# A two-layer decoder trunk on one core: weight slots of 4112 bytes, and where operands start modulo 256

## The chip, the core and the metric

The kernel runs on one core of one Trainium2 chip. The metric is the device time in microseconds (us) from start to end of one execution. The profile names the engines PE (TensorE, matmuls), PEld (TensorE's weight loads, which overlap its matmuls), DVE (VectorE), ACT (ScalarE), POOL (GpSimd) and SP (SyncE, which here only issues DMAs). TensorE's clock was granted at 0.999 of its full 2.4 GHz over the profiled execution.

## What is computed

Two decoder layers over 512 tokens of width 1024, in float32. Layer 0 mixes tokens with a chunkwise mLSTM, layer 1 with differential attention; both attend to a memory of 256 tokens, and both end in a SwiGLU feed-forward part 2816 wide:

```python
for i in range(DEPTH):
    h = rmsnorm(x, norm1[i])
    mix, xq = mlstm_mixer(h, ...) if i % 2 == 0 else diff_attention(h, positions, ...)
    xo = memory_cross_attention(xq, mem, mem_norm[i], w_mem_kv[i], xq_norm[i], xk_norm[i])
    x = x + jnp.concatenate([mix, xo], axis=-1) @ w_out[i]
    h = rmsnorm(x, norm2[i])
    gu = h @ w_gate_up[i]
    x = x + (jax.nn.silu(gu[..., :FFN_HIDDEN]) * gu[..., FFN_HIDDEN:]) @ w_down[i]
```

## The kernel before

**Three products for one.** All big products (the input projections, w_out, gate and up, down) run on TensorE in the type float32r. To keep float32's precision, each weight tile and each activation tile is split into a rounded high part and the rest, and three matmuls stand for one: high weight by high activation, high weight by low activation, low weight by high activation. A weight tile is 128 output columns by up to 8 blocks of 128 rows. It comes by DMA into one of four raw slots (`w_raw`), POOL (or ACT and DVE) splits it into `w_hi` and `w_lo`, and PE reads it there.

**Dense tiles** (`tile`, line 1946 is the helper `mm`): for each of 8 blocks k, three matmuls of 128x512. The operand that streams through the array (the moving one) is `Hh[:, k]` or `Hl[:, k]` (the normed tokens) or `Ah[:, k]` or `Al[:, k]` (the mixers' and the feed-forward part's outputs); the operand that is loaded into it first is a 128x128 block of `w_hi` or `w_lo`. There are 3120 such matmuls, and 192 more with only 256 moving columns (the memory's keys and values). `slot_of(n)` says in which of three slots of `w_hi` and `w_lo` tile n stands; most tiles alternate between slots 0 and 1.

**Pairs** (`pair`, line 2284): 16 of the 22 hidden blocks of each layer compute gate and up together, as seven products of quarter size (a Strassen-like scheme) over sums of activations (`tc_hi`, `tc_lo`) and sums of weights. Each product q takes 4 blocks of weights, starting at block `4 * q` (q is permuted a little in layer 1), and each block takes three matmuls of 128x256: 84 a pair, 2688 in all. The 28 blocks of the seven products lie in the same memory as the three slots: blocks 0 to 7 in slot 0, 8 to 15 in slot 1, 16 to 23 in slot 2, and 24 to 27 behind it.

**What PE does meanwhile.** Every matmul needs its own weight load, and the next load runs while the present matmul streams. So TensorE reads two places of SBUF at once: the moving rows of matmul i, and the weights of matmul i + 1.

**Where the operands lie.** Tensors are placed in SBUF in the order in which the function `sb` is called, each at the next multiple of 32 bytes. All the big ones were a multiple of 256 bytes long, so that they start alike modulo 256 (addresses are bytes within a partition):

| tensor | start before | modulo 256 | start after | modulo 256 |
|---|---|---|---|---|
| Hh, Hl | 17536, 33920 | 128 | the same | 128 |
| Ah, Al | 50304, 66688 | 128 | 50400, 66784 | 224 |
| w_raw | 83072 | 128 | 83168 | 224 |
| w_hi, w_lo | 99456, 113792 | 128 | 99616, 114208 | 32 |
| tc_hi, tc_lo | 169152, 197824 | 192 | 169632, 198304 | 160 |
| cn (constants), ones | 128128, 132896 | 128, 32 | 128608, 133376 | 96, 0 |
| tmp0, tmp1 | 154688, 156768 | 64, 96 | 155168, 157248 | 32, 64 |

In this text the **distance** is the start of the moving operand less the start of the weights loaded meanwhile, modulo 256. The step from one block to the next is 512 bytes for weights and 2048 or 1024 for moving rows, so that within a tile the distance stays the same. Before, it is 0 for every dense matmul and 64 for every matmul of a pair.

The lines that the change touches: the allocation of `w_hi` and `w_lo` and their views (`wq_hi`, `wq_lo` by block, `w_hi`, `w_lo` by slot), and four places that read or write a quarter's blocks: `weight_low` on POOL (line 748) and on DVE (line 1704), `weight_hi` on ACT (line 1099) and the matmul in `pair` (line 2284).

Of the kernel before, what the change touches and what calls it, by code (L numbers as in the profile page):

```python
# [25 lines left out]
F32 = mybir.dt.float32  # L26
F32R = mybir.dt.float32r
I32 = mybir.dt.int32
ALU = mybir.AluOpType
ACT = mybir.ActivationFunctionType  # L30
AX = mybir.AxisListType

P = 128
# [25 lines left out]
SPLIT = 3  # L59
# [60 lines left out]
HI_ENTRY = [4, 6, 0, 1, 5, 2, 3]  # L120
TOKENS = 13
SHARED = 2


def bq_tile(c):
# [138 lines left out]
def hybrid_trunk(nc, x_t, mem_t, positions, wt, wg_cols, a_gate_b, b_lambda, prm_cols, con, out):  # L264
    ctx = ExitStack()
    with ctx:
        def sb(name, shape, dt=F32, scope=ctx):
            return scope.enter_context(nc.sbuf_tensor(name, shape, dt))
# [7 lines left out]
        xT = sb("xT", [P, KD, SEQ])  # L276
        Hh = sb("Hh", [P, KD, SEQ], F32R)
        Hl = sb("Hl", [P, KD, SEQ], F32R)
        Ah = sb("Ah", [P, 8, SEQ], F32R)
        Al = sb("Al", [P, 8, SEQ], F32R)  # L280
        w_raw = sb("w_raw", [P, RAW, 8, P])
        wq_hi = sb("w_hi", [P, 28, P], F32R)
        wq_lo = sb("w_lo", [P, 28, P], F32R)
        w_hi = wq_hi[:, 0:8 * SPLIT].rearrange("p (s k) m -> p s k m", k=8)
        w_lo = wq_lo[:, 0:8 * SPLIT].rearrange("p (s k) m -> p s k m", k=8)
        cn = sb("cn", [P, N_CON])
        ones = sb("ones", [P, P])
        gcol = sb("gcol", [P, N_PRM])
# [229 lines left out]
        s_round = sem("s_round")  # L518
# [68 lines left out]
        def pair_source(n, q):  # L587

            gate, up = w_raw[:, n % RAW], w_raw[:, (n + 1) % RAW]
            return (gate[:, 0:4], W_SUM[1], W_SUM[0], W_SUM[2], gate[:, 4:8], W_SUM[3], up[:, 4:8])[q]  # L590
# [106 lines left out]
        def _(pool):  # L697
# [6 lines left out]
            for i in range(4):  # L704
                w = slice(2 * i, 2 * i + 2)
# [14 lines left out]
            for i in range(0, 4, 2):  # L720
                w = slice(i, i + 2)
# [23 lines left out]
            def weight_low(n, p, q):  # L745
                b = block_of(pair_at(n)[0], q)
                pool.wait_ge(s_round, weight_round(p, q))
                nc.gpsimd.tensor_tensor(wq_lo[:, b:b + 4], pair_source(n, q), wq_hi[:, b:b + 4].bitcast(F32),  # L748
                                        ALU.subtract).then_inc(s_low_p, 1)

            for n in range(2, N_TILES):
# [11 lines left out]
                if after_pairs(n):  # L763
                    l, s = after_pairs(n)
# [35 lines left out]
        def _(act):  # L800
# [266 lines left out]
            def ffn(l):  # L1067
# [17 lines left out]
                def weight_hi(s, i, q):  # L1085

                    n, p, b = seg_base(l, s) + 2 * i, pair_number(l, s, i), block_of(l, q)
                    if q in (0, 4, 6):
                        m = n + (q == 6)
                        act.wait_ge(w_in[m % RAW], (m // RAW + (m % RAW > 0)) * 16)  # L1090
                    else:
                        act.wait_ge(s_add, 4 * p + {1: 2, 2: 1, 3: 3, 5: 4}[q])
                    if i and q == 6:
                        act.wait_ge(dense_done, n)
                    elif i:
                        act.wait_ge(product, 6 * (p - 1) + q + 1)
                    else:
                        act.wait_ge(dense_done, n - 1 + q // 2 if q < 4 else n - KD + 1)
                    nc.scalar.activation(wq_hi[:, b:b + 4], pair_source(n, q), ACT.Copy).then_inc(s_round, 1)  # L1099

                def shared_hi(n):

# [215 lines left out]
        def _(dve):  # L1318
# [330 lines left out]
            def ffn(l):  # L1649
# [50 lines left out]
                def weight_low(s, i, q):  # L1700

                    n, p, b = seg_base(l, s) + 2 * i, pair_number(l, s, i), block_of(l, q)
                    dve.wait_ge(s_round, weight_round(p, q))
                    nc.vector.tensor_tensor(wq_lo[:, b:b + 4], pair_source(n, q), wq_hi[:, b:b + 4].bitcast(F32),
                                            ALU.subtract).then_inc(s_low_v, 1)

                def pair(s, i):
# [236 lines left out]
        def _(pe):  # L1944
# [317 lines left out]
            def pair(l, s, i):  # L2262

                p = pair_number(l, s, i)
                for q in range(7):
                    if q in P_LO:
                        pe.wait_ge(s_low_p, len(P_LO) * p + P_LO.index(q) + 1)
                    else:
                        pe.wait_ge(s_low_v, low_count(p, q))
                    if q == 4:  # L2270
                        pe.wait_ge(gate_read, 2 * p + 1)
                    elif q > 4:
                        pe.wait_ge(joined, joined_of(p, q - 3))
                    elif p and q == 0:
                        pe.wait_ge(gate_read, 2 * p)
                    elif p and q == 3 and i > plain_pairs(s):
                        pe.wait_ge(dense_free, seg_base(l, s) + 2 * i)
                    elif p and q < 3:
                        pe.wait_ge(joined, joined_of(p - 1, (1, 4)[q - 1]))
                    out_ = PS[:, Q_BANK[q], 0:HALF_T]  # L2280
                    b = block_of(l, q)
                    for k in range(4):
                        for j, (w, a) in enumerate(((wq_hi, tc_hi), (wq_hi, tc_lo), (wq_lo, tc_hi))):
                            last = nc.tensor.matmul(out_, w[:, b + k], a[:, q, k], start=q < 4 and k == 0 and j == 0,  # L2284
                                                    stop=k == 3 and j == 2, skip_group_check=q > 3)
                    last.then_inc(dense_done if q == 6 else product, 2 if q == 6 else 1)

# [328 lines left out]
```

## Time and profile before

| | |
|---|---|
| time, median of 2 runs | 1202.85 us (1202.53 to 1203.17) |
| profiled execution | 1204.02 us, its span 1202.2 us |
| PE busy | 1196.8 us, 100% of the span |
| PEld busy | 1032.9 us, 86% |
| POOL busy | 857.4 us, 71% |
| DVE, ACT busy | 755.9 us, 63%; 502.4 us, 42% |
| DMA | 117.43 MB, mean 98 GB/s |

A row of a grouped view gives line, engine, operation, output and inputs by the program's names, the shape, the count, the total busy time and the mean duration of one. Matmuls overlap: one is recorded from its start until its last result is written, and the next has started long before. So a matmul's duration is longer than the time from one start to the next, and it is the second that adds up to the span.

### The profile page before, as it was taken

The numbers are of one execution on the slowest core, as the hardware profiler recorded it, in microseconds if no ns is written. First come the engines' busy times: TensorE is split into PE (matmuls) and PEld (weight loads), VectorE is DVE, ScalarE is ACT, GpSimd is POOL, SyncE is SP. The second block draws the span as 40 slices with busy tenths as digits, with TensorE's granted clock in tenths as the row PEclk, the third lists the DMA queues.
The fourth block names the chain that finished last, engine by engine and source line by source line (L and its number), as shares of the span: only waits on it lengthen the run. The fifth ranks groups of instructions, "written<-read, shape, count | busy, mean of one in ns | idle before, by whom it ended". The sixth has DMA issues, their size and how long they took to land.

```text
span 1202.2 us, 18736 instructions
## 1 busy us (share of the span) xinstructions
PE 1196.8 (100%) x6998; PEld 1032.9 (86%) x6998; DVE 755.9 (63%) x1099; ACT 502.4 (42%) x1012; POOL 857.4 (71%) x873
## 2 busy tenths in 40 slices
PE   9999999999999999999999999999999999999998
PEld 7888887788889998899888777778888899889997
DVE  7954434645737991599335888874674599348931
ACT  7522456733203551355231666644431255125510
POOL 7998433566878996699676444445688799669965
PEclk9999999999999999999999999999999999999999
DMA  7234211132223333233433222232232333322332
GB/s 282 92 123 157 71 36 53 53 106 79 92 83 106 106 106 123 88 106 106 126 103 97 80 71 71 64 80 69 71 100 79 118 106 107 105 89 98 115 105 85
DMA packets 35097, 117.43 MB, mean 98 GB/s; under 512 B 4417, under 2 KB 4930, under 8 KB 34886
## 3 DMA queue, kind: packets, MB, share of 16 engines
q1 hardware_dynamic: 33416, 112.83, 29.2%
q10 hardware_dynamic: 1598, 3.51, 1.2%
q8 instruction: 51, 0.84, 0.3%
q14 instruction: 32, 0.26, 0.1%
HBM read 111.07 MB, written 2.11 MB: 94 GB/s over the span
## 4 chain that ended last, share of the span: by engine, by line
PE 97%; DVE 1%; ACT 1%; issue 0%; ACTq 0%; POOL 0%; POOLq 0%
PE PS L1946 69%; PE PS L2284 26%; PE PS L2385 1%; DVE Al L1564 0%; PE PS L2194 0%; PE PS L2413 0%; PE PS L2354 0%; DVE nmB L1850 0%; PE PS L2019 0%; PE PS L2346 0%; PE PS L2338 0%; DVE PB L1862 0%; ACT tmp L1010 0%; ACT tmp L1018 0%; DVE PB L1861 0%
## 5 line engine op out<-in xcount | busy, mean ns | idle before, releaser
L783 POOL TENSOR_TENSOR w_lo<-w_raw,w_hi 128x256 fp32r<-128x256 f32 (+1 forms) x516 | 394.7, 796 | 11.0
L778 POOL TENSOR_SCALAR w_hi<-w_raw 128x1024 fp32r<-128x1024 f32 (+2 forms) x132 | 142.1, 1076 | 283.4 <-PE PS L1946 275.0
L2284 PE MATMUL PS<-tc_hi,w_hi 128*128 128x256 f32 x896 | 250.9, 280 | 0.0
L2284 PE MATMUL PS<-tc_hi,w_lo 128*128 128x256 f32 x896 | 250.0, 279 | 0.0
L2284 PE MATMUL PS<-tc_lo,w_hi 128*128 128x256 f32 x896 | 250.0, 279 | 0.0
L1946 PE MATMUL PS<-Hh,w_hi 128*128 128x512 f32 x560 | 229.3, 410 | 0.0
L1946 PE MATMUL PS<-Hl,w_hi 128*128 128x512 f32 x560 | 219.1, 391 | 0.0
L1946 PE MATMUL PS<-Hh,w_lo 128*128 128x512 f32 x560 | 219.0, 391 | 0.0
L1946 PE MATMUL PS<-Ah,w_hi 128*128 128x512 f32 (+1 forms) x544 | 208.0, 382 | 0.1
L1946 PE MATMUL PS<-Ah,w_lo 128*128 128x512 f32 (+1 forms) x544 | 205.0, 377 | 0.0
L1946 PE MATMUL PS<-Al,w_hi 128*128 128x512 f32 (+1 forms) x544 | 204.9, 377 | 0.0
L2284 PEld LDWEIGHTS PS<-tc_hi,w_lo 128*128 128x128 f32 x896 | 168.5, 188 | 0.0
L2284 PEld LDWEIGHTS PS<-tc_hi,w_hi 128*128 128x128 f32 x896 | 168.2, 188 | 0.2
L2284 PEld LDWEIGHTS PS<-tc_lo,w_hi 128*128 128x128 f32 x896 | 167.6, 187 | 0.2
L1619 DVE TENSOR_TENSOR xT<-xT,PS 128x512 f32<-128x512 f32 x64 | 43.9, 687 | 159.4 <-PE PS L1946 159.4
L1946 PEld LDWEIGHTS PS<-Hh,w_hi 128*128 128x128 f32 x560 | 105.6, 189 | 27.6 <-issue 7.8
L1946 PEld LDWEIGHTS PS<-Hh,w_lo 128*128 128x128 f32 x560 | 105.4, 188 | 22.8
L1946 PEld LDWEIGHTS PS<-Hl,w_hi 128*128 128x128 f32 x560 | 105.7, 189 | 20.2 <-issue 1.0
L748 POOL TENSOR_TENSOR w_lo<-tmp,w_hi 128x512 fp32r<-128x512 f32 x64 | 107.7, 1700 | 17.9 <-ACT w_hi L1099 17.9
L1946 PEld LDWEIGHTS PS<-Ah,w_hi 128*128 128x128 f32 x544 | 102.3, 188 | 20.7 <-issue 1.5
L1946 PEld LDWEIGHTS PS<-Ah,w_lo 128*128 128x128 f32 x544 | 102.3, 188 | 19.0
L1946 PEld LDWEIGHTS PS<-Al,w_hi 128*128 128x128 f32 x544 | 102.4, 188 | 18.6 <-issue 0.5
(300 smaller groups left out, 1805.5 us busy)
## 6 DMA issues: line engine op xcount, KB each, us to landing
w_raw<-in_wt_dram SPq DMA_DIRECT2D x181, 512.0 KB, 3.6
w_raw<-in_wt_dram SPq DMA_DIRECT2D x16, 384.0 KB, 3.0
w_raw<-in_wt_dram SPq DMA_DIRECT2D x8, 448.0 KB, 3.3
QKR<-QKP ACTq DMA_DIRECT2D x24, 128.0 KB, 4.8
xT<-in_x_t_dram SPq DMA_DIRECT2D x8, 256.0 KB, 4.8
out_dram<-xT SPq DMA_DIRECT2D x8, 256.0 KB, 2.0
mT<-in_mem_t_dram SPq DMA_DIRECT2D x1, 1024.0 KB, 9.5
cn<-in_constants_dram SPq DMA_DIRECT2D x1, 594.5 KB, 6.9
```

Source lines behind the costliest of these rows:

```text
L748: nc.gpsimd.tensor_tensor(wq_lo[:, b:b + 4], pair_source(n, q), wq_hi[:, b:b + 4].bitcast(F32), ALU.subtract).then_inc(s_low_p, 1)
L778: nc.gpsimd.tensor_scalar(w_hi[:, sl, 0:nk], w_raw[:, raw, 0:nk], 0.0, 1.0, ALU.add, ALU.mult).then_inc(w_round, 1)
L783: lo = nc.gpsimd.tensor_tensor(w_lo[:, sl, w], w_raw[:, raw, w], w_hi[:, sl, w].bitcast(F32), ALU.subtract)
L1619: nc.vector.tensor_tensor(xT[:, k], xT[:, k], PS[:, bank], ALU.add).then_inc(dense_free, 1)
L1946: return nc.tensor.matmul(out_, a, b, start=start, stop=stop)
L2284: last = nc.tensor.matmul(out_, w[:, b + k], a[:, q, k], start=q < 4 and k == 0 and j == 0, stop=k == 3 and j == 2, skip_group_check=q > 3)
L2385: last = nc.tensor.transpose(PS[:, 2 + u % 2, k * P:(k + 1) * P], PB[:, 0, W_OFF[u] + k * P:W_OFF[u] + (k + 1) * P], ident)
```

## The change

The change puts three unused tensors between the operands (96 bytes ahead of `Ah`, 64 ahead of `w_hi`, 192 ahead of `w_lo`), and makes the weight slots 4112 bytes long instead of 4096, so that slot s starts 16 s bytes later modulo 256. The quarters of a pair keep their blocks, and follow the slots. With that the distances are:

| moving operand | before | after, slot 0, 1, 2 |
|---|---|---|
| Hh, Hl | 0 | 96, 80, 64 |
| Ah, Al | 0 | 192, 176, 160 |
| tc_hi, tc_lo (blocks 0-7, 8-15, 16-23, 24-27) | 64 | 128, 112, 96, 80 |

No instruction is added or taken away, and on no engine does one move: the order of instructions, their shapes and their waits are the same. Only addresses differ, those of the tensors behind `w_lo` too (all by 480 bytes).

```diff
+W_STEP = 8 * P + 4
...
         Hl = sb("Hl", [P, KD, SEQ], F32R)
+        sb("shift_a", [P, 24])
         Ah = sb("Ah", [P, 8, SEQ], F32R)
         Al = sb("Al", [P, 8, SEQ], F32R)
         w_raw = sb("w_raw", [P, RAW, 8, P])
-        wq_hi = sb("w_hi", [P, 28, P], F32R)
-        wq_lo = sb("w_lo", [P, 28, P], F32R)
-        w_hi = wq_hi[:, 0:8 * SPLIT].rearrange("p (s k) m -> p s k m", k=8)
-        w_lo = wq_lo[:, 0:8 * SPLIT].rearrange("p (s k) m -> p s k m", k=8)
+        sb("shift_hi", [P, 16])
+        wf_hi = sb("w_hi", [P, SPLIT * W_STEP + 4 * P], F32R)
+        sb("shift_lo", [P, 48])
+        wf_lo = sb("w_lo", [P, SPLIT * W_STEP + 4 * P], F32R)
+
+        def tile_slots(ap):
+
+            full = ap[:, 0:SPLIT * W_STEP].rearrange("p (s x) -> p s x", x=W_STEP)
+            return full[:, :, 0:8 * P].rearrange("p s (k m) -> p s k m", m=P)
+
+        def quarter_blocks(ap):
+
+            first = [(b // 8) * W_STEP + (b % 8) * P for b in range(0, 28, 4)]
+            return [ap[:, f:f + 4 * P].rearrange("p (k m) -> p k m", m=P) for f in first]
+
+        w_hi, w_lo = tile_slots(wf_hi), tile_slots(wf_lo)
+        wq_hi, wq_lo = quarter_blocks(wf_hi), quarter_blocks(wf_lo)
...
-                            last = nc.tensor.matmul(out_, w[:, b + k], a[:, q, k], start=q < 4 and k == 0 and j == 0,
+                            last = nc.tensor.matmul(out_, w[b // 4][:, k], a[:, q, k], start=q < 4 and k == 0 and j == 0,
```

The other edits write `wq_hi[b // 4]` for `wq_hi[:, b:b + 4]`, and the same for `wq_lo`, in the three places named above.

## Rows read from the trace of the kernel before

**Rows 1.** The page: busy time by engine, and the chain that ended last.
```profile
PE 1196.8 (100%) x6998; PEld 1032.9 (86%) x6998; DVE 755.9 (63%) x1099; ACT 502.4 (42%) x1012; POOL 857.4 (71%) x873
...
PE 97%; DVE 1%; ACT 1%; issue 0%; ACTq 0%; POOL 0%; POOLq 0%
```

**Rows 2.** The chain in order of time (start us, us, what): its longest pieces.
```profile
377.26 79.15 PE PS L2284 x672
456.41 43.56 PE PS L1946 x192
```

**Rows 3.** PE's groups, shapes apart, whole span: count, busy us, mean ns.
```profile
L1946 PE MATMUL PS<-Al,w_hi 128*128 128x256 f32 x64 | 18.1, 282 | 0.0
...
L1946 PE MATMUL PS<-QK 128*128 128x256 f32 x12 | 3.2, 379 | 0.0
L1946 PE MATMUL PS<-Hh,wg 128*128 128x512 f32 x8 | 3.2, 404 | 0.0
...
L1946 PE MATMUL PS<-QK,KZ 128*128 128x256 f32 x4 | 1.2, 379 | 0.0
```

**Rows 4.** The same, 300 to 324 us: dense tiles of gate and up alone.
```profile
L1946 PE MATMUL PS<-Hh,w_lo 128*128 128x512 f32 x36 | 14.0, 389 | 0.0
L1946 PE MATMUL PS<-Hh,w_hi 128*128 128x512 f32 x36 | 14.0, 389 | 0.0
L1946 PE MATMUL PS<-Hl,w_hi 128*128 128x512 f32 x36 | 14.0, 389 | 0.0
```

**Rows 5.** The same, 380 to 455 us: pairs alone.
```profile
L2284 PE MATMUL PS<-tc_hi,w_hi 128*128 128x256 f32 x213 | 59.6, 280 | 0.0
L2284 PE MATMUL PS<-tc_hi,w_lo 128*128 128x256 f32 x213 | 59.4, 279 | 0.0
L2284 PE MATMUL PS<-tc_lo,w_hi 128*128 128x256 f32 x213 | 59.4, 279 | 0.0
```

**Rows 6.** The same, 283.19 to 283.3 us: the last matmuls before `ones` is loaded.
```profile
L1946 PE MATMUL PS<-Hh,w_lo 128*128 128x512 f32 x1 | 0.4, 397 | 0.0
L1946 PE MATMUL PS<-Hl,w_hi 128*128 128x512 f32 x1 | 0.4, 389 | 0.0
```

**Rows 7.** The same, 651.7 to 651.8 us: the last before `tmp1` is loaded.
```profile
L1946 PE MATMUL PS<-Hh,w_lo 128*128 128x512 f32 x1 | 0.4, 396 | 0.0
```

**Rows 8.** The same, 650.1 to 650.2 us: the last before `tmp0` is loaded.
```profile
L1946 PE MATMUL PS<-Hh,w_lo 128*128 128x512 f32 x1 | 0.4, 388 | 0.0
```

**Rows 9.** The same, 456.2 to 458.1 us: the first dense matmuls behind the pairs.
```profile
L1946 PE MATMUL PS<-Ah,w_hi 128*128 128x512 f32 x3 | 1.2, 398 | 0.0
L1946 PE MATMUL PS<-Al,w_hi 128*128 128x512 f32 x3 | 1.2, 388 | 0.0
L1946 PE MATMUL PS<-Ah,w_lo 128*128 128x512 f32 x2 | 0.8, 394 | 0.0
```

**Rows 10.** Stretches: POOL's busy us (count), clock, DMA share, GB/s, in pairs.
```profile
380.00:450.00 70.00, 66.56 (x43) 1.00 0.30 106
```

More of the change, by code:

```diff
@@ L747, in weight_low @@
                 pool.wait_ge(s_round, weight_round(p, q))
-                nc.gpsimd.tensor_tensor(wq_lo[:, b:b + 4], pair_source(n, q), wq_hi[:, b:b + 4].bitcast(F32),
+                nc.gpsimd.tensor_tensor(wq_lo[b // 4], pair_source(n, q), wq_hi[b // 4].bitcast(F32),
                                         ALU.subtract).then_inc(s_low_p, 1)
@@ L1098, in weight_hi @@
                         act.wait_ge(dense_done, n - 1 + q // 2 if q < 4 else n - KD + 1)
-                    nc.scalar.activation(wq_hi[:, b:b + 4], pair_source(n, q), ACT.Copy).then_inc(s_round, 1)
+                    nc.scalar.activation(wq_hi[b // 4], pair_source(n, q), ACT.Copy).then_inc(s_round, 1)
                 def shared_hi(n):
@@ L1703, in weight_low @@
                     dve.wait_ge(s_round, weight_round(p, q))
-                    nc.vector.tensor_tensor(wq_lo[:, b:b + 4], pair_source(n, q), wq_hi[:, b:b + 4].bitcast(F32),
+                    nc.vector.tensor_tensor(wq_lo[b // 4], pair_source(n, q), wq_hi[b // 4].bitcast(F32),
                                             ALU.subtract).then_inc(s_low_v, 1)
```

## The prediction

> **What bounds the kernel now.** I read the page first: PE is busy for 1196.8 of 1202.2 us, and 97% of the chain that ended last is PE [rows 1]. So the time is the sum of the steps from one matmul's start to the next, and no other engine's speed matters as long as it stays under PE's. The change touches addresses alone. It can therefore move the time only through how long such a step takes, and the next views are there to measure it.
>
> The chain in order of time gives it directly. 192 dense matmuls take 43.56 us, 226.9 ns each; 672 matmuls of pairs take 79.15 us, 117.8 ns each [rows 2]. The grouped views give the same steps in another form. A dense matmul is recorded with 389 ns [rows 4] and one of a pair with 279 to 280 [rows 5]: both are the step plus 162 ns, the time from the last column's entry to the last result. So 162 ns off a recorded duration gives the step, also for a single matmul. At 2.4 GHz (the clock granted here is 1.00) 512 columns take 213.3 ns and 256 take 106.7. What is over, I call the surplus:
>
> - dense, 512 columns, distance 0: 226.9 - 213.3 = about 13.5 ns;
> - dense, 256 columns, distance 0: 282 - 162 - 106.7 = about 13.3 ns [rows 3];
> - pairs, 256 columns, distance 64: 117.8 - 106.7 = 11.1 ns.
>
> The first two say that the surplus does not grow with the columns: it belongs to the weight load, one a matmul. The last two differ in the tensors and in the distance, and by 2.3 ns. For comparison, plain float32 matmuls stream each column for twice as long: 256 columns take 379 - 162 = 217 ns, 213.3 and 3.7 more by this reckoning, and the same at distance 0 (`QK` by `QK`) and at 192 (`QK` by `KZ`) [rows 3]. So there is no effect of the distance where the moving rows come at half the speed, and for float32r some 10 ns of a surplus of 11 to 13.5 could in principle be saved.
>
> **The change part by part.** The sum is made against the profiled execution, whose span is 1202.2 us; its own time is 1204.02, and the median of the runs shown is 1202.85, so I add each term to 1202.85.
>
> *Dense matmuls away from distance 0.* There are 3312. If a distance other than 0 gives them the pairs' surplus, each saves 2.3 ns: 3312 x 2.3 = 7.6 us less. Bounds: at best the surplus falls to that of float32, 10 ns less each, 33 us; at worst it is that of the single loads below.
>
> *Distance 96.* Single loads show other distances. When `ones` (distance 96) is loaded under a matmul with `Hh`, that matmul is recorded with 397 ns, its neighbour with 389 [rows 6]; it is so at all four places where this load stands in a stretch of dense tiles, of which one is shown. `tmp1` (distance 32) gives 396 [rows 7], `tmp0` (distance 64), behind the same instructions, 388 [rows 8]. So 64 is good and 32 and 96 cost 8 ns more. By the table of slots, 718 dense loads (H tiles in slot 0) and 768 loads of pairs (blocks 16 to 23) come to distance 96. Were every one 8 ns longer, that is 1486 x 8 = 11.9 us more. But a single step is not a steady one. Behind the pairs the distance is 0 at once, yet the first eight steps read 398, 388 and 394 ns [rows 9], and then 389: the stall depends on what went before, and settles. I take half, 6 us more, and keep 0 and 12 as bounds.
>
> *Pairs leave distance 64.* They go to 128, 112, 96 and 80. If they fell to distance 0's surplus, 2688 x 2.3 = 6.2 us more; if they keep theirs, 0. The one row at distance 128 is the load of `wg` under `Hh`, 404 ns [rows 3], in the kernel's first 16 us, where every load is disturbed. I take 0.
>
> *Slots that differ.* Where the distance changes by 16 from tile to tile, and four times in a pair, the steps may have to settle anew. In the whole program the weights' start modulo 256 now changes 248 times between neighbours. Rows 9 price one settling: 3 x 398 + 3 x 388 + 2 x 394 - 8 x 389 = 34 ns [rows 9], for a change of shape and of 64 bytes. 248 x 34 ns = 8.4 us is the upper bound, 0 the lower; with a step of only 16 bytes I take 2.
>
> *Everything else.* ACT, DVE and POOL write and read the same number of bytes at shifted addresses, and the DMA's rows are as long as before. I cost it at nothing: in the dense tiles PE runs without a gap, and all of these engines have slack there. The pairs are the exception: POOL is busy for 66.56 of 70 us [rows 10]. A pair can get shorter by no more than 4.9% before PE waits for POOL, which caps what pairs could give at 2688 x 117.8 ns x 0.049 = 15.5 us. A POOL that got 5% slower by its new addresses would hold the pairs up; nothing in the rows speaks for that.
>
> Sum: -7.6 + 6 + 0 + 2 = 0.4 us, 1203 us.
>
> **A rule of the skill.** The rows say that a matmul's surplus goes with the weight load and was 2.3 ns smaller at distance 64 [rows 2, 3]. The Trainium skill, "TensorE: Matmul & The Clock Gate", section "What happens when you issue a matmul", states that TensorE has two independent SBUF read ports and that loading the next tile's weights doesn't steal read bandwidth from the running matmul. By it the distance would be of no account, and the sum would be 0. The rows agree for float32 and not quite for float32r.
>
> **The rivals.**
>
> *Most of the stall goes.* The two reads collide at distance 0 in a way that the new distances avoid. For it: a surplus of 13.5 ns against float32's 3.7 [rows 3, 4], and one that varies with the distance at all. Against: distance 64 is away from 0 and saves only 2.3 ns; no step in the steady stretches is shorter. Price: 33 us in the dense tiles, 15.5 in the pairs (POOL's cap): 1154 us; half of it 1179. It is faster by over 2% as soon as the mean step falls by 4 ns over the 6000 float32r matmuls. Chance 0.19.
>
> *The new distances stall more.* The 8 ns of rows 6 and 7 are steady, and hold for 80, 176 and 192 too. For it: distances 32 and 96 are the only ones in these rows that are far from 0 and 64, and both are bad; the settled state of distance 0 is then a lucky one. Against: 388 ns at distance 64 [rows 8]. Price: 6000 x 8 ns = 48 us, 1251 us; it decides (over 2% slower) from a mean of 4 ns on, 1227. Chance 0.13.
>
> *The address is of no account.* Steps of dense matmuls and pairs differ for another reason (the tensors' place in SBUF, or the pattern of the products), and rows 6 and 7 are particular to float32 weights. Then nothing moves: 1202.85 us. Chance 0.18.
>
> *The forecast:* small effects of both signs, 1190 to 1220 us. Chance 0.50.
>
> **How the numbers follow.** Over 2% is 24 us, about what a measurement of this kernel can tell from no change. Faster by over 2%: 0.19; slower: 0.13; within 2%: 0.50 + 0.18 = 0.68. The predicted time is the forecast's sum, 1203 us. For eight in ten the range takes in the nearer half of each outer rival: from 1168 us (a mean step 6 ns shorter) to 1226. The likeliest case's own range is 1190 to 1220.
>
> **What the profile would show.** Instructions, their order, the chain's shares (97% PE) and POOL's load stay. The dense groups in a stretch of gate and up tell the first two terms: 387 ns in place of 389 if a distance other than 0 gives the pairs' surplus, 397 in the tiles of slot 0 with H if distance 96 costs 8 ns steadily, 379 if the stall goes. A tiles (192, 176) and H tiles (96, 80) will differ if the distance matters. The pairs' 279 to 280 ns tell the third; a first matmul in each tile that is longer than the later ones, the fourth. The prediction is wrong if the mean moves by over 4 ns, or if PE starts to wait for POOL's w_lo in the pairs.

## The result, and the profile after

The changed kernel takes 1219.47 us (median of 2 runs, 1218.67 to 1220.26) against 1202.85 us: a ratio of 1.0138, with an interval of 1.0109 to 1.0168. So it is 16.6 us slower, a difference under the 2% that the prediction's cases are divided by, and outside the noise. The profiled execution took 1220.26 us, its span is 1218.5 us at a granted clock of 0.999.

The page of after (busy time by engine, then the chain that ended last by engine) answers to [rows 1]:

```profile
PE 1213.1 (100%) x6998; PEld 1036.0 (85%) x6998; DVE 741.6 (61%) x1099; ACT 504.8 (41%) x1012; POOL 855.2 (70%) x873
...
PE 98%; DVE 1%; DMA 0%; POOL 0%; ACT 0%; issue 0%; ACTq 0%; SPq 0%; POOLq 0%
```

Same instructions, and the chain is still PE's for 98%: PE's busy time has grown by 16.3 us and the span by 16.3. The pieces of the chain in order of time (start, us, what) answer to [rows 2]:

```profile
381.72 80.16 PE PS L2299 x672
461.88 44.62 PE PS L1961 x192
```

672 matmuls of pairs went from 79.15 to 80.16 us, 117.8 to 119.3 ns a step. 192 dense ones with `A` went from 43.56 to 44.62 us, 226.9 to 232.4 ns. The grouped view of 470 to 500 us, dense tiles with `A` alone (PE's groups, shapes apart: count, busy us, mean ns; idle before), has 395 ns where [rows 4] have 389:

```profile
L1961 PE MATMUL PS<-Al,w_hi 128*128 128x512 f32 x44 | 17.4, 395 | 0.0
L1961 PE MATMUL PS<-Ah,w_lo 128*128 128x512 f32 x44 | 17.4, 395 | 0.0
```

With `H` the two slots can be told apart in the view of one line's instructions of after (306 to 309 us, a tile in slot 0, distance 96; durations as least/median/most), and in the grouped view of 300 to 304 us (a tile in slot 1, distance 80):

```profile
L1961 PE MATMUL PS<-Hl,w_hi x5: 399/399/399, 305.7 to 308.5; 128*128 128x512 f32 x5
L1961 PE MATMUL PS<-Hh,w_lo x5: 392/392/397, 305.9 to 308.7; 128*128 128x512 f32 x5
L1961 PE MATMUL PS<-Hh,w_hi x5: 392/394/394, 306.1 to 308.9; 128*128 128x512 f32 x5
```
```profile
L1961 PE MATMUL PS<-Hh,w_lo 128*128 128x512 f32 x7 | 2.7, 392 | 0.0
L1961 PE MATMUL PS<-Hl,w_hi 128*128 128x512 f32 x6 | 2.4, 393 | 0.0
L1961 PE MATMUL PS<-Hh,w_hi 128*128 128x512 f32 x6 | 2.4, 392 | 0.0
```

The three matmuls of a block are now unequal and repeat: 399, 394, 392 at distance 96. Their mean less 162 is 233; at distance 80 it is 230. And the pairs, whole span, against 279 to 280 in [rows 5]:

```profile
L2299 PE MATMUL PS<-tc_lo,w_hi 128*128 128x256 f32 x896 | 253.0, 282 | 0.0
L2299 PE MATMUL PS<-tc_hi,w_lo 128*128 128x256 f32 x896 | 252.6, 282 | 0.0
L2299 PE MATMUL PS<-tc_hi,w_hi 128*128 128x256 f32 x896 | 252.5, 282 | 0.0
```

Adding up the steps from start to start, out of the start times of all PE instructions in both traces (neighbouring pairs of matmuls on `w_hi` or `w_lo` whose step is under 300 ns), gives where the time came from:

| matmuls | before: distance, steps, mean ns | after: distance, mean ns | us |
|---|---|---|---|
| `A`, 512 columns | 0, 1404, 227.1 | 192: 233.1; 176: 231.8; 160: 233.3 | +7.6 |
| `H`, 512 columns | 0, 1475, 227.9 | 96: 233.5; 80: 230.3; 64: 229.3 | +5.6 |
| `A`, 256 columns | 0, 187, 120.9 | 192: 117.4; 176: 119.8; 160: 117.5 | -0.5 |
| pairs, 256 columns | 64, 2688, 117.8 | 128: 118.7; 112: 119.8; 96: 119.5; 80: 118.4 | +3.7 |

Together +16.5 us, for 16.3 of the span; all other steps together got 0.2 us shorter. So the whole loss is in the steps of float32r matmuls, and most of it in the dense tiles. Of the 5.6 us of `H`, 3.7 fall on the tiles at 96 (658 of the steps), and 1.8 on those at 80 and 64.

### The profile page after: what moved, and what is told of

It reads as the page before. It is cut to its first block, busy times and chain, and to the rows that moved or that the text cites. A ratio compares the mean times of both kernels' runs of the same rounds, so it can differ in the third digit from the quotient of the medians.

```text
span 1218.5 us, 18736 instructions
## 1 busy us (share of the span) xinstructions
PE 1213.1 (100%) x6998; PEld 1036.0 (85%) x6998; DVE 741.6 (61%) x1099; ACT 504.8 (41%) x1012; POOL 855.2 (70%) x873
## 4 chain that ended last, share of the span: by engine, by line
PE 98%; DVE 1%; DMA 0%; POOL 0%; ACT 0%; issue 0%; ACTq 0%; SPq 0%; POOLq 0%
PE PS L1961 69%; PE PS L2299 26%; PE PS L2400 1%; PE PS L2209 0%; PE PS L2428 0%; DMA w_raw<-in_wt_dram 0%; PE PS L2369 0%; DVE nmB L1865 0%; PE PS L2034 0%; PE PS L2361 0%; PE PS L2353 0%; DVE PB L1877 0%; PE PS L2169 0%; PE PS L2172 0%; DVE PB L1876 0%; DVE PS L1863 0%
## 5 line engine op out<-in xcount | busy, mean ns | idle before, releaser
L2299 PE MATMUL PS<-tc_lo,w_hi 128*128 128x256 f32 x896 | 253.0, 282 | 0.0
L2299 PE MATMUL PS<-tc_hi,w_lo 128*128 128x256 f32 x896 | 252.6, 282 | 0.0
L1961 PE MATMUL PS<-Al,w_hi 128*128 128x512 f32 (+1 forms) x544 | 207.4, 381 | 0.0
```

What stands on the lines that cost most here:

```text
L1961: return nc.tensor.matmul(out_, a, b, start=start, stop=stop)
L2299: last = nc.tensor.matmul(out_, w[b // 4][:, k], a[:, q, k], start=q < 4 and k == 0 and j == 0, stop=k == 3 and j == 2, skip_group_check=q ...
```

## The experiments

Two theories at first. **Distance:** the step of a float32r matmul depends on the distance of its moving rows from the weights that are loaded meanwhile, modulo 256. **Place:** it depends on where one operand lies by itself (modulo 256, or in SBUF), or on the slots that differ by 16 bytes; then shifting everything, or one side, would do as much. Edits are against the kernel before unless another is named.

### Everything shifted alike: all_moved

```diff
+        sb("shift_all", [P, 40])
         xT = sb("xT", [P, KD, SEQ])
```

> The kernel before with one unused tensor of 160 bytes ahead of everything: Hh, Ah and the weights all start at 32 modulo 256, where the changed kernel's weights start; the distances stay 0 (dense) and 64 (pairs). Distance theory: 1203 us, dense matmuls 389 ns, pairs 279 to 280. Place theory (weights at 32 are what costs): about as slow as the changed kernel, 1219, dense matmuls 394 or more.

1202.70 us, ratio 0.9999 (0.9987 to 1.0010). All operands lie 160 bytes further on, no distance changed, and the durations stayed within 1 ns (grouped view, whole span):

```profile
L2285 PE MATMUL PS<-tc_hi,w_lo 128*128 128x256 f32 x896 | 250.0, 279 | 0.0
...
L1947 PE MATMUL PS<-Hh,w_lo 128*128 128x512 f32 x560 | 218.8, 391 | 0.0
...
L1947 PE MATMUL PS<-Ah,w_lo 128*128 128x512 f32 x480 | 186.9, 389 | 0.0
```

A shift of everything by 160 bytes is of no account.

### Only H against its weights: ahead_of_a

```diff
+        sb("shift_a", [P, 24])
         Ah = sb("Ah", [P, 8, SEQ], F32R)
```

`A` and the weights move together by 96 bytes, so `A` stays at 0 and the pairs at 64, while `H`'s distance becomes 160.

> One part of the change alone: 96 bytes ahead of Ah. A and the weights move together, so only H tiles change their distance, from 0 to 160; A stays at 0 and the pairs at 64. Distance theory: A tiles 389 ns and pairs 279 to 280 as before; H tiles at the changed kernel's figure for distance 160, a step of about 233, recorded 395: 1680 matmuls x about 6 ns = 10 us more, 1213. Place theory (Ah at 224 is what costs): A tiles slower, H tiles not.

1211.77 us, ratio 1.0075 (1.0045 to 1.0104). Whole span, grouped:

```profile
L1947 PE MATMUL PS<-Hh,w_lo 128*128 128x512 f32 x560 | 221.8, 396 | 0.0
...
L1947 PE MATMUL PS<-Ah,w_lo 128*128 128x512 f32 x480 | 186.9, 389 | 0.0
```

`H` rose from 391 to 396 ns and `A` stayed at 389, though `A` and the weights had moved and `H` had not. `H`'s mean step is 234.0 ns, 6.1 more than before; by the 1475 steps that is 9.0 us, and the kernel lost 9.1. That is distance, not place.

### The changed kernel without slots of 4112 bytes: no_slot_step

```diff
-W_STEP = 8 * P + 4
+W_STEP = 8 * P
...
-        sb("shift_lo", [P, 48])
+        sb("shift_lo", [P, 64])
...
+        sb("shift_cn", [P, 16])
```

(Against the kernel after.) All slots now lie alike: `H` at 96, `A` at 192, pairs at 128.

> The change with slots of 4096 bytes again and everything else of it: all H tiles at distance 96, all A tiles at 192, all pairs at 128, no change of the distance between neighbours. Distance theory: each group reads what it reads at that distance in the changed kernel, steps of 233.5 (H), 233 (A) and 118.7 (pairs): 3 ns more on the half of the H matmuls that were at 80, 1 ns more on A's at 176, 1 ns less on three quarters of the pairs: about 1219, like the changed kernel. Slot theory (it is the changes between neighbours that cost): most of the 16 us comes back, 1203 to 1208.

1222.80 us, ratio 1.0166 (1.0137 to 1.0196), 3.3 us above the changed kernel where the same had been expected. The steps themselves came as expected: `H` 233.4 ns, `A` 233.3, pairs 118.7. So the loss needs no steps between slots; with them it is even less, since slot 1's distances 80 (230.3) and 176 (231.8) are better than 96 and 192.

### The distances measured by themselves: probe

The model is left out but for a copy of x; PE alone runs series of 48 float32r matmuls, three for each of 8 blocks, twice, as in a tile. Each series has one pair of offsets, at 512 or 256 columns (the generator of one series; its first lines are left out):

```diff
+            for r in range(2):
+                for k in range(8):
+                    for j, (W, o, M) in enumerate(((Wh, wo, Mh), (Wh, wo, Ml), (Wl, wl, Mh))):
+                        yield (PS[:, r, 0:n], W[:, o + k * P:o + (k + 1) * P], M[:, mo + k * n:mo + (k + 1) * n],
+                               k == 0 and j == 0, k == 7 and j == 2)
```

> This kernel leaves out all of the model: it copies x to the output, and PE runs nothing but series of 48 dense-like matmuls (two tiles of 24, in the three-product pattern), each series from a source line of its own. Series 1 to 18: 512 columns, the weights moved by 0, 0, then 0 to 240 bytes in steps of 16 with the moving rows fixed (distance 0 downwards: 0, 240, 224, ...). Then the same 16 with 256 columns. Then 8 with the moving rows moved by 0 to 224 in steps of 32 and the weights fixed (distance upwards), then three with both moved by 32, 96 and 160 (distance 0), then distance 0 again. The distance theory (the step from one matmul to the next depends on the moving operand's start less the weights', modulo 256, and on nothing else of the place): the recorded durations at 512 columns are 389 ns at distance 0 in all places, about 392 to 396 at 64 to 192 as in the changed kernel's tiles (step 230 at 80, 233 at 96, 232 at 176, 233 at 192, plus 162), and a series with the moving rows moved equals the one with the weights moved the other way. The place theory (where weights or rows start modulo 256 or 64 matters, each for itself): the last three series differ from 389, and the two sweeps don't mirror each other. If both are wrong and the change slowed PE through the other engines' traffic, all series read the same.

It took 442.67 us, clock 1.00. Rows of the grouped view (one line of code is one series; 512 columns): line 319 at distance 0, 323 at 192, 329 at 96, 331 at 64, all four by an offset of the weights; 354 at 96 by an offset of the moving rows; 360 with both offset by 96.

```profile
L329 PE MATMUL PS<-Mh,Wh 128*128 128x512 f32 x16 | 6.4, 399 | 0.0
L354 PE MATMUL PS<-Ml,Wh 128*128 128x512 f32 x16 | 6.4, 399 | 0.0
...
L323 PE MATMUL PS<-Ml,Wh 128*128 128x512 f32 x16 | 6.3, 396 | 0.0
...
L331 PE MATMUL PS<-Mh,Wh 128*128 128x512 f32 x16 | 6.3, 394 | 0.0
...
L329 PE MATMUL PS<-Mh,Wl 128*128 128x512 f32 x16 | 6.3, 394 | 0.0
...
L329 PE MATMUL PS<-Ml,Wh 128*128 128x512 f32 x16 | 6.3, 392 | 0.0
L331 PE MATMUL PS<-Mh,Wl 128*128 128x512 f32 x16 | 6.3, 392 | 0.0
...
L319 PE MATMUL PS<-Mh,Wh 128*128 128x512 f32 x16 | 6.2, 389 | 0.0
...
L360 PE MATMUL PS<-Ml,Wh 128*128 128x512 f32 x16 | 6.2, 389 | 0.0
...
L331 PE MATMUL PS<-Ml,Wh 128*128 128x512 f32 x16 | 6.2, 388 | 0.0
```

399, 394, 392 at 96: the same three numbers as in the changed kernel's tile. It does not matter which operand is moved, and moved together they are back at 389. No other engine works during these series, so the two reads of PE are enough to make it. The settled mean steps, from start to start, in ns:

| distance | 0 | 16 | 32 | 48 | 64 | 80 | 96 | 112 | 128 | 144 | 160 | 176 | 192 | 208 | 224 | 240 |
|---|---|---|---|---|---|---|---|---|---|---|---|---|---|---|---|---|
| 512 columns | 226.7 | 226.7 | 233.3 | 233.3 | 228.9 | 229.8 | 233.4 | 233.4 | 233.5 | 233.3 | 234.3 | 232.0 | 233.3 | 233.3 | 233.4 | 226.7 |
| 256 columns | 120.0 | 119.9 | 116.8 | 116.6 | 113.3 | 118.1 | 119.9 | 120.0 | 118.7 | 120.0 | 118.7 | 118.7 | 113.3 | 117.8 | 118.4 | 118.3 |

At 512 columns distance 0 and its two neighbours are the best in this probe, where each series comes behind its neighbour in the table; the neighbours do not keep that place (probe3 and slots_4112 below). All dense tiles stood at 0 before. 64 and 80 are in the middle, and the other eleven cost 5 to 8 ns. With 256 columns the order is another one, and 0 is among the worst. Distance 64 gives 113.3 ns here and 117.8 in the kernel before; the next two probes ask why.

### Period, unequal distances: probe2

The same with distances to 512, with one offset for the high and another for the low operands, and with 256 columns entered in other ways. One series of it, of 256 bytes for both moving operands (the five arguments of `seq` are here the offsets of the high and low moving rows and of the high and low weights, in elements of 4 bytes, and the columns):

```diff
+            for o, w, a, first, end in seq(64, 64, 0, 0, 512): nc.tensor.matmul(o, w, a, start=first, stop=end)
```

> Again a kernel that leaves out all of the model and runs series of 48 matmuls, each from a line of its own. The first probe read 113.3 ns a step at 256 columns and distance 64, the pairs in the whole kernel 117.8 at the same distance. The two differ in how far the low tensors lie from the high ones: 0 modulo 512 in the pairs, 256 in the probe. Here the tensors lie 0 modulo 512 apart. Series: distances 0 to 480 in steps of 32 at 512 columns and at 256; distance 64 with the low activations, the low weights or both 256 bytes further; then at both widths from distance 0 the low weights alone, the low activations alone, or both, 32 to 224 bytes apart. Theory that the period is 512 and the low tensors' place counts: distance 64 with 0 modulo 512 apart reads 117.8 and with 256 apart 113.3, and the sweep differs between d and d + 256. Theory that the period is 256 and several settled cycles exist, of which what ran before picks one: d and d + 256 read alike where the start is alike, and distance 64 reads 113.3 or 117.8 depending on what stands ahead. If unequal distances of high and low can settle lower than 32 cycles over 512 columns (226.7 ns), some of the last series read below 388.6 ns recorded.

753.45 us. Line 326 is distance 256 at 512 columns; lines 337 and 345 are 64 and 320 at 256 columns (the view of one line):

```profile
L326 PE MATMUL PS<-Mh,Wh 128*128 128x512 f32 x16 | 6.2, 389 | 0.0
```
```profile
L337 PE MATMUL PS<-Ml,Wh x16: 279/279/279, 240.3 to 245.6; 128*128 128x256 f32 x16
```
```profile
L345 PE MATMUL PS<-Ml,Wh x16: 279/279/279, 285.9 to 291.2; 128*128 128x256 f32 x16
```

The period is 256 bytes: 256 reads as 0 and 320 as 64, at both widths, to the ns. Moving the low tensors by 256 against the high ones changes nothing. Different distances for high and low gave 228.9 to 233.3 ns at 512 columns, none under 226.7. And 64 at 256 columns is 117.8 ns now, in all eight variants, as in the kernel; in the first probe it was 113.3. The high and low tensors lay 256 bytes modulo 512 apart there, both rows and weights; two of the eight variants have just that, and four more have it for one of the two, so it is not the reason. What ran before differs, and the next probe tries it by itself.

### What ran before: probe3

343 series: targets of 24 matmuls at 256 columns or 21 at 512, each behind an entry of another distance, width or length. Two entries and the target behind them, lines 469 to 471 (the sixth argument is the number of matmuls):

```diff
+            for o, w, a, first, end in seq(0, 0, 0, 0, 512, 12): nc.tensor.matmul(o, w, a, start=first, stop=end)
+            for o, w, a, first, end in seq(8, 8, 0, 0, 256, 12): nc.tensor.matmul(o, w, a, start=first, stop=end)
+            for o, w, a, first, end in seq(16, 16, 0, 0, 256, 24): nc.tensor.matmul(o, w, a, start=first, stop=end)
```

> Third probe, model left out, no other engine at work: 343 series without a gap, each from a line of its own. It asks what picks the settled cycle. At 256 columns and distance 64 the first probe read 113.3 ns a step (16 cycles over) and the second 117.8 (26.7 over), and hi-to-lo offsets and the period were ruled out. (a) 15 matmuls of 512 columns at distance 0, 16 or 240, then 24 of 256 columns at each of 16 distances. (b) 12 of 512 columns at distance 0, then 3 or 12 of 256 at each distance, then 24 of 256 at 64 or at 192. (c) 12 of 256 columns at eight distances, then 21 of 512 at 0, 16, 64 or 80. Theory of several settled cycles: the same target reads 113.3 behind some entries and 117.8 behind others, and stays there. Theory that a distance has one settled step: every target reads the same whatever stands ahead, and the difference between the probes was something else. If 512 columns at distance 0 has a second, shorter cycle, some of (c) reads a step below 226.7.

923.61 us. The same target, distance 64 at 256 columns, behind 12 matmuls at distance 32 (line 471) and at 48 (line 474), in the view of one line:

```profile
L471 PE MATMUL PS<-Ml,Wh x8: 276/276/276, 442.8 to 445.2; 128*128 128x256 f32 x8
```
```profile
L474 PE MATMUL PS<-Ml,Wh x8: 279/279/284, 449.7 to 452.2; 128*128 128x256 f32 x8
```

113.3 against 117.8 ns, from the same code at the same distance: one distance has more than one settled cycle, and the entry picks it. As in the kernel before, behind 512 columns at distance 0, the targets gave: 64: 117.8; 192: 117.8; 0 and 128: 120.0; 112: 113.3. Distance 112 was at 113.3 behind 512 columns at 0, 16 and 240 alike (line 337: 275 ns once settled), where the first probe, coming from 128, had 120.0 at it. It is a candidate for the pairs. At 512 columns distance 0 always settled at 226.7 to 227.0, 64 at 228.9 (once 233.3), 80 at 231.1; 16 gave 231.0 to 232.3 in all 24 series here and 226.7 in the first probe. Distance 240, which the first probe had at 226.7 too, was entered 16 times, by 15 matmuls behind 256 columns: it went to 226.7 in three, to 233.3 in two, and to 236.3 to 237.1 in eleven, the longest steady steps of this study. One series of each end (lines 404 and 386, the same code):

```profile
L404 PE MATMUL PS<-Ml,Wh x5: 388/388/388, 291.7 to 294.4; 128*128 128x512 f32 x5
```
```profile
L386 PE MATMUL PS<-Ml,Wh x5: 397/398/402, 234.4 to 237.2; 128*128 128x512 f32 x5
```

So only distance 0 was good at 512 columns behind every entry tried.

### The pairs at 112: pairs_112

```diff
+        sb("shift_cn", [P, 8])
         cn = ...
...
-        tc_hi = sb("tc_hi", [P, 7, 4, HALF_T], F32R, scope=sT)
-        tc_lo = sb("tc_lo", [P, 7, 4, HALF_T], F32R, scope=sT)
+        tc_hi = sb("tc_hi", [P, 28 * HALF_T + 64], F32R, scope=sT)[:, 4:4 + 28 * HALF_T].rearrange("p (q k n) -> p q k n", q=7, k=4)
+        tc_lo = sb("tc_lo", [P, 28 * HALF_T + 64], F32R, scope=sT)[:, 4:4 + 28 * HALF_T].rearrange("p (q k n) -> p q k n", q=7, k=4)
```

Dense tiles stay at 0.

> The kernel before with the pairs' activations moved alone: tc_hi and tc_lo at distance 112 instead of 64, dense tiles at 0 as before. In the third probe 256 columns at distance 112, entered from 512 columns at distance 0 (as the pairs are), settled at 113.3 ns a step, where distance 64 settled at 117.8. Theory that the entry picks the settled cycle and PE's reads are all that counts: pairs recorded with 275 ns in place of 279.5, 2688 x 4.4 ns = 12 us less, 1191. Against it: POOL is busy for 95% of a pair now, 9.5 of 9.9 us, and a pair at 113.3 ns lasts 9.52 us, so PE should begin to wait for w_lo; a wait may also throw the cycle out (the second probe, coming from distance 96, settled at 120 at this same distance, which would give 1209). Between: some stages at 113.3 and some not, 1194 to 1205.

1199.21 us, ratio 0.9967 (0.9954 to 0.9979): the fastest kernel of this study, 3.7 us under the one before. First PE's groups over the whole span, then the stretches (busy us and count of one engine's row; clock, DMA share, GB/s), POOL's of 400 to 445 us and DVE's of the same:

```profile
L2285 PE MATMUL PS<-tc_hi,w_hi 128*128 128x256 f32 x896 | 248.7, 278 | 1.6 <-DVE tmp L1727 0.4
L2285 PE MATMUL PS<-tc_lo,w_hi 128*128 128x256 f32 x896 | 246.8, 275 | 0.0
```
```profile
400.00:445.00 45.00, 43.93 (x29) 1.00 0.33 118
```
```profile
400.00:445.00 45.00, 40.78 (x56) 1.00 0.33 118
```

The step came down from 117.8 to 113.3 ns, 275 recorded for 279. That would be 2688 x 4.5 = 12 us, and 3.7 came. A pair (84 matmuls) should take 84 x 113.3 = 9.52 us. The first (9.56) and the last (9.52) of a stage do, but those between start 9.84 us apart, against 9.89 before (the second of a stage even 9.95 to 10.06). In each of these PE stops once, ahead of the product q = 5, with a step of 291 to 537 ns and some longer ones right behind it; the other products run at 113.3 ns a step. The stop ends as DVE's sum of two products (tmp, line 1727) does, and that sum stands on DVE behind the next pair's w_lo, which needs ACT's w_hi and POOL's sums of weights. POOL is busy for 43.93 of 45 us, exactly as in the same stretch of the kernel before. The chain of pairs_112 at the beginning of the first stage of pairs shows who leads (start, us, what):

```profile
378.39 1.43 POOL w_lo L749
...
379.98 1.55 POOL tmp L737
...
381.60 1.64 POOL tmp L739
383.24 1.28 POOL tmp L742
```

### The same with POOL relieved: pairs_112_dve, and the control pairs_64_dve

```diff
-V_LO = [0, 3, 4, 5, 6]
-V_ENTRY = [4, 6, 0, 5, 3]
-P_LO = [1, 2]
+V_LO = [0, 1, 3, 4, 5, 6]
+V_ENTRY = [4, 6, 0, 1, 5, 3]
+P_LO = [2]
...
-                    pool.wait_ge(s_low_p, 2 * p)
+                    pool.wait_ge(s_low_p, p)
...
+                if p:
+                    pool.wait_ge(s_low_v, low_count(p - 1, 1))
...
+                    low(1)
```

(Against pairs_112.) One of the low quarters of a pair goes from POOL to DVE. The control has the same edit with the pairs at 64.

> pairs_112 took 4.4 ns off a step in the first pair of each stage, but the pairs behind it lasted 9.84 us instead of 9.52, POOL busy for 96% of them. Here the low part of the second quarter's weights (q = 1) goes from POOL to DVE, in pairs at distance 112. POOL gets about 1.7 us a pair less, DVE 0.9 us more, and DVE is busy for 90% now. POOL theory (POOL held the pairs at 9.84 us): pairs of 9.52 to 9.65 us, 32 x 0.2 to 0.32 = 6 to 10 us less than pairs_112, 1189 to 1193. If DVE becomes the bound in its place: 9.8 us or more, 1199 or worse. If the pairs in pairs_112 were long because a wait threw the cycle out: steps of 120 appear here too.

> The same move of one low part from POOL to DVE without any change of address: pairs at distance 64. At 64 it is PE that sets the pairs (117.8 ns a step, 9.89 us a pair), so that a lighter POOL should bring nothing: 1203. If this too gets to 1199 or below, the gain of pairs_112_dve isn't due to the address.

pairs_112_dve: 1200.27 us, ratio 0.9973 (0.9962 to 0.9985); pairs_64_dve: 1206.29 us, ratio 1.0019 (1.0009 to 1.0030). PE's group in each (112 first), and with distance 112 POOL's and DVE's stretch:

```profile
L2288 PE MATMUL PS<-tc_hi,w_hi 128*128 128x256 f32 x896 | 248.0, 277 | 5.5 <-DVE tmp L1729 5.1 <-DVE w_lo L1707 0.4
```
```profile
L2287 PE MATMUL PS<-tc_hi,w_hi 128*128 128x256 f32 x896 | 250.6, 280 | 2.2 <-DVE tmp L1728 1.9 <-DVE w_lo L1706 0.3
```
```profile
400.00:445.00 45.00, 37.05 (x24) 1.00 0.34 118
```
```profile
400.00:445.00 45.00, 42.89 (x64) 1.00 0.34 118
```

POOL is down to 37.05 of 45 us, and the later pairs of a stage now take 9.52 us each: so it was POOL's load that had held them. But DVE is at 42.89, and the first three pairs of a stage take 9.87 to 10.5 us; PE now idles for 5.1 us on DVE's tmp. The expectation for POOL relieved, 1189 to 1193 us, missed; the other one, DVE as the bound, is nearer. The chain of pairs_112_dve around the first pair of the first stage runs through DVE's w_lo, so DVE seems to enter the stage late:

```profile
376.34 1.29 DVE w_lo L1707 x2
...
378.59 3.44 DVE w_lo L1707 x2
...
382.07 9.86 PE PS L2288 x84
```

The control was expected at 1203 us and pays 3.5 us for the move, without the shorter step in most of its pairs (five of the 32 have it, see the last section). Against the control distance 112 is worth 6.0 us; without the move, 3.7. The rest of the 12 us is still behind POOL and DVE.

### Other distances in the kernel: pairs_128 and dense_64

```diff
+        sb("shift_cn", [P, 16])
```

ahead of `cn`, for the pairs at 128, and for the dense tiles at 64 (`cn` and `tc_hi` move along by the same 192 bytes, so the pairs are still at 64):

```diff
+        sb("shift_hi", [P, 48])
         wq_hi = sb("w_hi", [P, 28, P], F32R)
```

> The pairs' part of the change alone and without slot steps: 64 bytes ahead of cn, so that all pairs lie at distance 128; dense tiles at 0. Distance theory: pairs at the probes' 118.7 ns a step in place of 117.8 (recorded 281), 2688 x 0.9 = 2.4 us more, 1205; dense unchanged at 389. If the pairs' loss in the changed kernel came from the steps between their blocks instead, 1203.

> My prediction's first term tried directly: 192 bytes ahead of w_hi, so that all dense tiles lie at distance 64, where the pairs are; the pairs stay at 64. The prediction said 2.3 ns less for each of 3312 dense matmuls, 7.6 us less, 1195. The probes say that 512 columns at distance 64 take 228.9 ns, 2.2 more than at 0: 3120 x 2.2 = 6.9 us more, less 0.4 for the 192 narrow ones: 1209.

pairs_128: 1208.97 us, ratio 1.0048 (1.0032 to 1.0064). dense_64: 1206.68 us, ratio 1.0032 (1.0019 to 1.0045). The longest piece of the chain in pairs_128, then a dense one in dense_64:

```profile
377.63 80.64 PE PS L2285 x672
```
```profile
457.81 43.96 PE PS L1947 x192
```

pairs_128 has a step of 80.64 / 672 = 120.0 ns, where no_slot_step, at the same distance, had 118.7: two cycles again, behind dense tiles at 0 here and at 192 there. The expected 1205 us had been worked out from 118.7 and missed; probe3 had read 120.0 at 128 behind 512 columns at 0. 2688 x 2.2 = 5.9 us; measured +6.1. In dense_64, 43.96 / 192 = 229.0 ns, 2.1 more than at 0, as the probe had it; `H` steps rose by 1.5 to 229.4. By 1404 and 1475 steps that is 2.7 + 2.2 = 4.9 us; measured is +3.8 (1209 had been expected), as a part of the pairs, entered from 512 columns at 64, fell into the cycle of 113.3 (mean 117.2).

### The slots alone: slots_4112

```diff
-        sb("shift_a", [P, 24])
...
-        sb("shift_hi", [P, 16])
...
+        sb("shift_cn", [P, 48])
```

(Against the kernel after.) Slots of 4112 bytes, dense tiles at 0, 240, 224 and pairs at 64, 48, 32, 16.

> The other part of the change alone: slots of 4112 bytes, with the first slot's distances as before. Dense tiles at distance 0 (slot 0), 240 (slot 1) and 224 (slot 2), pairs at 64, 48, 32 and 16. Distance theory with the probes' steps: 226.7 ns at 0 and at 240, 233.4 at 224 (230 matmuls, 1.5 us more); pairs between 116.6 (48) and 119.9 (16), in sum 0.5 to 1 us less; together 1203 to 1205. If a change of slot costs a settling of 34 ns each time, as my prediction bounded it, 8 us more: 1211.

1203.66 us, ratio 1.0006 (0.9995 to 1.0016). The steps are 228.3 (`H`, 0), 229.7 (`H`, 240), 227.2 and 227.8 (`A`), 233 at 224, and 116.7 to 118.6 in the pairs. That the time is the same is a balance: by the steps of both traces the dense tiles take 3.3 us more than before, and the pairs 2.0 less. Where tiles alternate between 0 and 240 in settled state, the steps read 226 and 227 across every change of slot, so a change of 16 bytes by itself costs nothing there. But at least eight whole tiles of slot 1 (distance 240) stand at 233 ns, as some series of probe3 did, among them the first dense tile of slot 1 behind each of the last two stages of pairs. One tile of each kind, both at 240 (grouped view, 89.5 to 94.5 and 136.5 to 141 us):

```profile
L1960 PE MATMUL PS<-Hl,w_hi 128*128 128x512 f32 x8 | 3.2, 398 | 0.0
```
```profile
L1960 PE MATMUL PS<-Hl,w_hi 128*128 128x512 f32 x7 | 2.7, 389 | 0.0
```

## Why the prediction was right or wrong

The time fell into the range of 1168 to 1226 us and into the forecast case's own 1190 to 1220, and within 2%. That is in good part luck: 1219.47 is half a microsecond inside the case's edge, the predicted 1203 was 16.5 us too low, and the largest term had the wrong sign. "Small effects of both signs" did not hold in its second half: all large terms had one sign. The mechanism was that of the second rival, at a third of its price. The range was also said to take in the nearer half of each outer rival, but it ends at 1226, below the 1227 from which the slower one begins.

**What bounds the kernel** held: PE's chain, no other engine, and the step from start to start as the thing to measure. 162 ns off a recorded duration gave steps that agree with the chain and with the start times.

**Dense tiles away from distance 0: -7.6 us. This step failed**, in its sign. It took the pairs' surplus at 64 (11.1 ns, 256 columns) for what any distance other than 0 gives at any width, since the surplus at distance 0 was 13.5 and 13.3 ns at both widths. At 512 columns distance 64 has 228.9 - 213.3 = 15.6 ns (probe), dense_64 lost 3.8 us where this step would have won 7.6, and no other distance is better than 0. In the changed kernel the dense matmuls away from 0, without those at 96, cost 7.6 (`A`), 1.8 (`H` at 80 and 64) and -0.5 us (`A`, 256 columns): 8.9 us more in place of 7.6 less. That is as much as the whole miss of 16.5 us; what the other terms were off by cancels. That distance 0 had the same surplus at two widths was a coincidence of that distance: at 64 it is 15.6 and 11.1.

**Distance 96: +8 ns each, of which half was taken, +6 us.** The size held: 3.7 us in the `H` tiles and 768 x 1.7 ns = 1.3 us in the pairs, 5.0 together. Its argument did not, and the half was right by luck. That [rows 9] settle says nothing of 96, since they settle at distance 0, where the good cycle is; 96 settles at the bad one, and the steady dense step is 6.7 ns longer, nearly the whole 8 of the single loads [rows 6]. The pairs at 96, 256 columns wide, lost only 1.7 ns each, and the two errors cancel. The single row at 64 [rows 8] misled: 388 stands also in the probe's cycle at 64, beside 394 and 392, and one recorded matmul is not the mean of its cycle. What was missing is a price like that of 96 for 176 and 192, which the second rival had ("hold for 80, 176 and 192 too").

**Pairs leave 64: 0, with a bound of 6.2.** Measured +3.7 (the 1.3 at distance 96 among them), inside the bound. The bound's price, distance 0's surplus for 2688 steps, is very near what pairs_128 lost (6.1); after the changed dense tiles the pairs settled in part at better cycles.

**Slots that differ: +2.** Near 0, as far as the runs can tell: slots_4112 is at 1.0006, an interval that reaches from -0.6 to 1.9 us, but that is a sum of several effects. In its settled dense stretches a change of slot costs nothing. In the changed kernel, where tiles of `H` alternate between 96 and 80, one at 96 averages 233.9 ns against the 233.4 of the settled distance: 0.5 ns a matmul.

**Everything else: 0** held. ACT, DVE and POOL kept their load within 2% (502.4 to 504.8, 755.9 to 741.6, 857.4 to 855.2 us). **The cap by POOL** was not touched by this change, but pairs_112 ran into it: a pair between the first and the last got shorter by 0.5%, not 4.9%. The cap was worked out from POOL's 3.44 us of idle time in [rows 10]. But 1.9 us of them are a single wait, ahead of the dense tile's `w_hi` (line 778), and 1.2 us are seven pauses of 0.17 us behind its last w_lo of a pair. From 400 to 445 us POOL is idle for 2.4% before and in pairs_112 alike: it had next to nothing to give.

**The rivals.** "The new distances stall more" had the right mechanism and sign; by the rows above its mean is 16.5 us over 5754 steps, 2.9 ns, under the 4 ns from which it would have decided. It had assumed 8 ns everywhere; it is 4.7 to 6.2 in the dense tiles but for distances 80 and 64 (2.4 and 1.4), and 1.4 in the pairs. "Most of the stall goes" is refuted for 512 columns, at multiples of 16 bytes: none of 16 distances is under 226.7 ns. For 256 columns it is half true, since 113.3 ns exist, 6.7 over the columns' 106.7. "The address is of no account" is refuted by ahead_of_a and the probe; and with it the Trainium skill's sentence ("TensorE: Matmul & The Clock Gate", "What happens when you issue a matmul") that loading the next weights takes no read bandwidth from the running matmul is not borne out here for float32r: moving one operand by 96 bytes costs 6.7 ns a matmul, and moving both nothing. For float32 the rows of [rows 3] agree with it.

**What the profile would show.** 397 for slot 0 with `H` came as a mean of 395 (399, 394, 392); `A` and `H` tiles did differ, in after by slots as well.

## What to carry to other kernels

Before moving operands of back-to-back float32r matmuls, measure a short series for each distance between moving rows and weights modulo 256, at the kernel's own number of columns and behind what runs before it in the kernel: the distance that is good at 512 columns behind every entry (0) is not the one at 256 (112 behind 512 columns, and 64 or 192 by chance). A distance that reads well behind one entry (240 at 512 columns) can be the worst of all behind another. Do not take one recorded instruction for a steady rate, nor a surplus measured at one width for another. When a step gets shorter, look first which engine feeds it: here two thirds of a gain of 12 us stayed behind POOL and the sums of DVE that wait for it.

## What the runs showed of the hardware

- The step of a float32r matmul with its own weight load depends on the start of the moving rows less that of the weights being loaded, modulo 256 bytes. The settled range is 226.7 to 237.1 ns at 512 columns and 113.3 to 120.0 at 256. Where both lie by themselves was of no account in any shift tried (all_moved, lines 359 to 361 of the probe).
- The state is periodic over a few matmuls (226, 227, 227 ns at distance 0; 232, 237, 231 at 96), and one distance can have more than one periodic state: at 256 columns 113.3 or 117.8 ns at 64, 113.3 or 120.0 at 112, 118.7 or 120.0 at 128; at 512 columns 226.7, 233.3 or 236.3 to 237.1 at 240. What ran before picks one, and it lasts: in pairs_64_dve the last five pairs of one stage took 9.52 us each in place of 9.89, though their distance is 64 as in the others.
- What inside the chip makes the two reads disturb each other was not tried and stays open; the runs show the distance, its period and the cycles alone. Distances that are no multiple of 16 bytes were not tried either.
